# Sums of squares spread over dense tiles, and each head's output norm one step later, in a two-block transformer kernel on one core

## The chip, the cores and the metric

The kernel runs on one core of one Trainium2 chip. The metric is the device time of one execution in microseconds (us), the median over several executions; less is better. The core's engines are TensorE (PE in the profile; its weight loads are PEld), VectorE (DVE), ScalarE (ACT), GpSimd (POOL) and SyncE (SP, which issues most of the loads).

## The reference

512 tokens of width 1024 go through two transformer blocks. The change lies in the first, in its gated delta rule. Cut to what matters:

```python
qkv = silu(causal_dwconv(dn_qkv, dn_conv_w))           # dn_qkv: columns of h @ w_in + b_in
q, k, vv = split(qkv, [1024, 2048])                     # 8 heads of 128 each
q = q * rsqrt(sum(q * q, -1) + 1e-6)
k = k * rsqrt(sum(k * k, -1) + 1e-6)
beta, g = sigmoid(dn_b), -exp(dn_a_log) * softplus(dn_a + dn_dt_bias)
# chunks of 64 tokens: G = cumsum(g); a unit lower triangular system per chunk
lmat = where(strict, beta * (k k^T) * decay, 0)
sol  = triangular_solve(eye + lmat, [v * beta, k * beta * exp(G)])
o    = scan over the chunks (state, attention with decay)
o = o * rsqrt(mean(o * o, -1) + 1e-6) * dn_norm_w * silu(z)   # the head's output norm
```

The rest of the first block (spatial gating, merging, layer norms, a mixture of 32 experts) and the whole second block (attention, a recurrence, a feed-forward part) are not touched.

## The kernel before

Activations lie with the width on the 128 partitions and the 512 tokens along the row. The input projection is cut into 72 *dense tiles* `("d", n)` of 128 output columns by 512 tokens. A tile is 24 matmuls with 512 moving columns: for each k of 0 to 7 the three products of `exact` (high by low, high by high, low by high part of fp32 numbers). `p_dense` issues them; it is a generator that yields after k = 3, so that a tile can be taken in two halves. Tiles 0 to 23 are q, k and v of the heads: ACT copies a tile out of PSUM (`s_evac`), DVE does the convolution (`v_qkv`, three SCALAR_TENSOR_TENSOR on BG), ACT the SiLU and, for q and k, the square (`s_silu`; squares go to ST for the first eight, to M for the last eight, and `sq_done` counts them).

`p_sums(r, bank)` adds the squares up over the partitions: for four squares `m = 4r + y` and four groups of 128 tokens it takes the square as the stationary operand and one column of ones as the moving one. So 16 matmuls of one column, which the trace holds as 32 records (each fp32 matmul is two). ACT waits for the filled tile `("nc", r)` before it writes the next four squares.

Every engine's program is written out by hand, in order, with semaphore waits. `p_qk`, `s_qk`, `v_qk`, `g_qk` are the first stage (tiles 0 to 11). Then the eight heads run in pairs: `weave` takes one step of head h and of head h + 1 in turn, then one half dense tile (`p_dense1` and its partners), on each engine separately. `p_head`, `v_head`, `s_head`, `g_head` are the steps of one head; step 1 of `p_head` is `kb`, step 2 `kk` and `dt`, step 3 `at`, step 4 `eg`, then eight steps without work for the heads on PE. In these DVE does the 16-row triangular inverse by substitution, for both heads of a pair at once: `v_sub_turn` (one STREAM_TRANSPOSE of ST) opens it and `v_sub_rows` are 28 small operations that each wait for the one before. At its end `v_sub_spread` gives `xt0`, which PE waits for (`x0`, transposes L276 of cst,ST).

The norm of a head's output is its *tail*: `p_tail_sums` (4 one-column matmuls, 8 records, tile `on`), `v_tail_sums` (mean plus epsilon, sm<-ps,sm), `s_tail` (square root), `v_tail_spread` (reciprocal, then a 128x512 product ST<-cst,sm), `p_tail_scale` (tile `os`, ST,cst with 512 columns), `v_tail` (BG<-BG,pc,ps, 128x512). The tail of head h - 2 is done inside the first steps of head h; those of heads 6 and 7 in `p_merge`.

PSUM has eight banks; `B.tile(key, bank)` names a tile, and `room(t)` makes PE wait until the bank's last tile was drained. Dense tiles use banks 0 and 1 beside the heads, a pair's heads banks 2 to 4 and 5 to 7 (`b0 = 2 + 3 * (h % 2)`).

Of the kernel before, what the change touches and what calls it, by code (L numbers as in the profile page):

```python
# [17 lines left out]
P = 128  # L18
D = 1024
T = 512  # L20
NT = 4
# [148 lines left out]
def build(nc, a, cst_d, rope_d, out):  # L170
    ctx = ExitStack()
    with ctx:
# [57 lines left out]
        def four(x):  # L230
            return x.rearrange("p (c t) -> p c t", c=4)
# [23 lines left out]
        def tt(E, o, x, y, op):  # L255
            return E.e.tensor_tensor(o, x, y, op)  # L256
# [14 lines left out]
        def mm(o, l, r, start=True, stop=True):  # L271
            return p.e.matmul(o, lhsT=l, rhs=r, start=start, stop=stop, skip_group_check=True)  # L272
# [16 lines left out]
        hTp = (HTH, HTL)  # L289

        def exact(o, l, r, start, stop):
            mm(o, l[0], r[1], start=start, stop=False)
            mm(o, l[0], r[0], start=False, stop=False)
            return mm(o, l[1], r[0], start=False, stop=stop)

        def room(t):
            for x in t.room:
                p.wait_ge(*x)
# [347 lines left out]

        def p_dense(n, bank, rhs, kind):
            p.wait_ge(*split_done(("d", n)))  # L650
            t = B.tile(("d", n), bank, nr=2 if n < 24 else 1)
            room(t)
            x, hi, lo = parts(("d", n))
            for k in range(8):
                p.wait_ge(*split_done((kind, k)))
                z = exact(t.at, (hi[:, k, :], lo[:, k, :]), (rhs[0][:, k, :], rhs[1][:, k, :]), k == 0, k == 7)
                if k == 3:
                    yield
            z.then_inc(t.filled)
            w_used[n // 4] = [t.full()]  # L660
# [68 lines left out]
        def sq_at(m):  # L729
            return ST[:, m % 4, :] if m < 8 else M[:, m % 4, :]  # L730

        def p_sums(r, bank):
            t = B.tile(("nc", r), bank)
            room(t)
            for y in range(4):
                m = 4 * r + y
                p.wait_ge(sq_done, m + 1)
                for i in range(NT):  # L740
                    z = mm(t.at[:, 4 * i + y:4 * i + y + 1], sq_at(m)[:, i * P:(i + 1) * P], ones[:, 0:1])
            z.then_inc(t.filled)

        def heads4(x, r):
            return x[:, :, 4 * (r // 2):4 * (r // 2) + 4]
# [136 lines left out]
        def s_prep2():  # L882
# [4 lines left out]
            s.wait_ge(*t.full())  # L887
            act(eGr, t.at[0:32, 0:P], ACT.Exp).then_inc(t.drained)

        def p_qk():  # L890
            for n in range(12):
                for _ in p_dense(n, n % 4, hTp, "T"):
                    pass
                if n == 2:
                    p_ab()
                elif n == 5:
                    p_prep1()
                    p_sums(0, 6)
                elif n == 9:
                    p_prep2()  # L900
                    p_sums(1, 7)
            p_beta(1, 6)

        def s_qk():
# [140 lines left out]
        def p_head(h):  # L1045
            LT, C, X, XT, Y, AT = sets[h % 2]
            KG, KD, VB, VN = LT, C, X, Y
            q4, k4, v4 = four(Qr[:, h, :]), four(Kr[:, h, :]), four(Vr[:, h, :])
            b0 = 2 + 3 * (h % 2)
            p.wait_ge(*B["rb"].free())  # L1050
            p.wait_ge(*B["br", h // 4].free())
            p_spread(("kb", h), b0, h, btr[h // 4])
            if h > 1:
                p_tail_sums(h - 2)
            yield
            p.wait_ge(silu_done, qk_of(h))
            p.wait_ge(*B["kb", h].free())
            p_products(("kk", h), b0 + 1, lambda c: k4[:, c, :], lambda c: Y[:, c, :])
            p.wait_ge(gm_done, h + 1)
            p_products(("dt", h), b0 + 2, lambda c: X[:, c, :], lambda c: ule)  # L1060
            yield
            p_products(("at", h), b0, lambda c: k4[:, c, :], lambda c: q4[:, c, :])
            if h > 1:
                p_tail_scale(h - 2)
            yield
            p_spread(("eg", h), b0 + 2, h, eGr)
            yield
            for _ in range(8):
                yield
            p.wait_ge(xt0_done, h + 1)  # L1070
            p_turn4(("x0", h), b0 + 1, XT)
            yield
            p.wait_ge(*B["x0", h].free())
            for n in range(3):
                p.wait_ge(lc_done[h % 2], 3 * (h // 2) + n + 1)
                if n:
                    p.wait_ge(*B["xx", h, n - 1].free())
                p_half(("y", h, n), b0, C, firsts(X, n))
                yield
                p.wait_ge(*B["y", h, n].free())  # L1080
                p_half(("xt", h, n), b0 + 2, Y, seconds(XT, n))
                yield
                if n < 2:
                    p.wait_ge(*B["xt", h, n].free())
                    p_turn4(("xx", h, n), b0 + 1, XT)
                    yield
            p_turn4(("kt", h), b0, k4)
            p.wait_ge(silu_done, v_of(h))
            p_turn4(("vt", h), b0 + 1, v4)
            yield  # L1090
            p.wait_ge(*B["kt", h].free())
            p.wait_ge(*B["xt", h, 2].free())
            p_products(("w", h), b0 + 2, lambda c: KG[:, c, :], lambda c: XT[:, c, :])
            yield
            p.wait_ge(*B["vt", h].free())
            p.wait_ge(*B["w", h].free())
            S = Y[:, 3, :]
            ob = B.tile(("o", h), b0)
            room(ob)
            for c in range(4):  # L1100
                n2 = 2 if c < 3 else 1
                t = B.tile(("s", h, c), b0 + 1 + c % 2, nw=n2, nr=n2)
                room(t)
                cs = slice(c * P, (c + 1) * P)
                if c:
                    p.wait_ge(*B["s", h, c - 1].free())
                    mm(t.at[:, 0:P], XT[:, c, :], VB[:, c, :], stop=False)
                    mm(t.at[:, 0:P], KG[:, c, :], S, start=False).then_inc(t.filled)
                    mm(ob.at[:, cs], S, q4[:, c, :], stop=False)
                else:  # L1110
                    mm(t.at[:, 0:P], XT[:, c, :], VB[:, c, :]).then_inc(t.filled)
                yield
                vn = VN[:, c % 2, :]
                p.wait_ge(*t.free(1))
                z = mm(ob.at[:, cs], vn, AT[:, c, :], start=c == 0)
                if c == 3:
                    z.then_inc(ob.filled)
                else:
                    mm(t.at[:, P:2 * P], KD[:, c, :], vn).then_inc(t.filled)
                yield  # L1120
# [4 lines left out]
        fd_done, of_done = sem("o_scale_spread"), sem("o_scale")  # L1125

        def p_tail_sums(h):
            t, z = B.tile(("on", h), 4 + 3 * (h % 2)), sets[h % 2][3]
            room(t)
            p.wait_ge(hsq_done, h + 1)  # L1130
            for c in range(4):
                i = mm(t.at[:, c:c + 1], z[:, c, :], ones[:, 0:1])
            i.then_inc(t.filled)

        def p_tail_scale(h):
            t = B.tile(("os", h), 4 + 3 * (h % 2))
            room(t)
            p.wait_ge(fd_done, h + 1)
            mm(t.at, ones, sets[h % 2][3].rearrange("p c t -> p (c t)")).then_inc(t.filled)
# [23 lines left out]
        def v_head(h):  # L1163
# [4 lines left out]
            v.wait_ge(*t.full())  # L1168
            v.wait_ge(silu_done, qk_of(h))
            tt(v, Y, k4, four(t.at), MUL).then_inc(t.drained)  # L1170
            if h > 1:
                v_tail_sums(h - 2)
            yield
            if h > 1:
                v_tail_spread(h - 2)
            yield
            t = B["kk", h]
            v.wait_ge(*t.full())
# [4 lines left out]
            v.wait_ge(*t.full())  # L1183
            tt(v, AT, four(t.at), C, MUL).then_inc(t.drained)
            if h > 1:
                v_tail(h - 2)
            yield
            t = B["eg", h]
            v.wait_ge(*t.full())
# [1 line left out]
            tt(v, q4, q4, four(t.at), MUL).then_inc(t.drained)  # L1191
            v_sub_take(h)
            yield
            for i0, i1 in ((1, 5), (5, 8), (8, 10), (10, 12), (12, 14), (14, 15), (15, DB)):
                if h % 2:
                    if i0 == 1:
                        v_sub_turn(h)
                    v_sub_rows(h, i0, i1)
                    if i1 == DB:
                        v_sub_back()  # L1200
                yield
# [40 lines left out]

        def s_head(h):
            LT, C, X, XT, Y, AT = sets[h % 2]
            if h > 1:
                s_tail(h - 2)
            yield
            t = B["dt", h]
            s.wait_ge(*t.full())
            act(C, four(t.at), ACT.Exp).then_inc(t.drained)  # L1250
            for _ in range(11):
                yield
            t = B["x0", h]
            s.wait_ge(*t.full())
# [81 lines left out]

        def p_dense1():
            for n in range(12, 24):
                half = p_dense(n, n % 2, hTp, "T")
                next(half)  # L1340
                yield
                if n == 18 or n == 22:
                    p_sums(2 if n == 18 else 3, 1)
                yield from half
                yield
            for n in range(24, 32):
                half = p_dense_tok(n, n % 2)
# [2328 lines left out]
```

## Time and profile before

| | |
|---|---|
| runs of before | 2186.38, 2188.93, 2196.76 us; median 2188.93 |
| the profiled execution | 2186.67 us; span 2184.8 us, granted TensorE clock 0.945 |
| PE busy | 1991.2 us, 91% of the span |
| DVE busy | 951.7 us (44%) |
| ACT busy | 654.0 us (30%) |
| POOL busy | 434.0 us (20%) |
| first block up to the experts | about 0 to 750 us |
| experts | about 750 to 1270 us |

A profile is one execution. A row's times are us from the span's start. "Granted clock" is the share of full speed at which TensorE was allowed to run; 1.00 is 2.4 GHz and 0.50 is 1.2 GHz.

### The profile page before, as it was taken

Reading aid. Unit: us, or ns where it says so; the run is one execution under the profiler, and the core shown is the slowest. Engines: PE = TensorE matmul, PEld = TensorE weight load, DVE = VectorE, ACT = ScalarE, POOL = GpSimd, SP = SyncE. Lnnn points to the kernel's source line nnn. Section 1 sums busy time; section 2 is a strip of 40 time slices with the busy share of each in tenths; the row PEclk is TensorE's granted clock in tenths of the full one; section 3 lists DMA queues with packets and bytes.
Section 4 is the critical chain, followed back from the end, with each engine's and each line's share of the span. In section 5 each row is a group of like instructions: output and inputs, shape, how many; then the busy total and the mean of one; then the engine's idle time right before and its main releaser. Section 6 shows DMA issues by size and latency. Waiting matters only on the chain.

```text
span 2184.8 us, 22949 instructions
## 1 busy us (share of the span) xinstructions
PE 1991.2 (91%) x9520; PEld 1442.1 (66%) x9520; DVE 951.7 (44%) x1382; ACT 654.0 (30%) x981; POOL 434.0 (20%) x310
## 2 busy tenths in 40 slices
PE   7999989999999889787787889998879899999999
PEld 5887878888877733332333347676746687888787
DVE  7674475542535622110111155845635883222332
ACT  4554422424333101000000133352226753222221
POOL 5432131423326011111110022311003120000121
PEclk9898999999999889898998999999979899999999
DMA  4861423123244589999999953111201134232210
GB/s 164 258 158 49 97 58 78 39 77 57 60 149 182 201 326 405 403 406 407 407 409 411 417 202 116 39 49 49 68 29 39 39 126 154 95 98 98 96 58 39
DMA packets 97654, 361.02 MB, mean 165 GB/s; under 512 B 9850, under 2 KB 34588, under 8 KB 85256
## 3 DMA queue, kind: packets, MB, share of 16 engines
q1 hardware_dynamic: 86800, 335.14, 42.9%
q0 software_dynamic: 8240, 19.00, 2.5%
q10 hardware_dynamic: 2504, 5.35, 0.7%
q8 instruction: 78, 1.28, 0.2%
q14 instruction: 32, 0.26, 0.0%
HBM read 338.74 MB, written 29.10 MB: 168 GB/s over the span
## 4 chain that ended last, share of the span: by engine, by line
PE 78%; DVE 11%; ACT 5%; issue 4%; DMA 1%; POOL 0%; ACTq 0%; SPq 0%; DVEq 0%; POOLq 0%
PE ps L272 74%; PE ps L276 3%; DVE ST L256 2%; PE ps L2080 2%; DVE H L262 1%; ACT ST L268 1%; ACT L268 1%; DVE WL L256 1%; DVE BG L262 1%; DVE ST L994 1%; ACT M L268 1%; DVE sm L3017 0%; DVE BG L256 0%; DMA BG<-h1d,toki 0%; DVE ML L256 0%
## 5 line engine op out<-in xcount | busy, mean ns | idle before, releaser
L272 PE MATMUL ps<-XH,WS 128*128 128x512 f32 x704 | 218.7, 392 | 0.0
L272 PE MATMUL ps<-HTH,WL 128*128 128x512 f32 x448 | 180.0, 402 | 0.0
L272 PE MATMUL ps<-W,BG 128*64 128x512 f32 x496 | 160.2, 618 | 1.0 <-issue 1.0
L272 PEld LDWEIGHTS ps<-XH,WS 128*128 128x128 f32 x704 | 133.5, 190 | 28.1
L2187 DVE COPY BG<-ps 128x512 f32<-128x512 f32 x32 | 22.1, 692 | 288.7 <-PE ps L272 288.7
L266 ACT ACTIVATE BG<-ps 128x512 f32<-128x512 f32 x48 | 28.5, 595 | 373.5 <-PE ps L2080 339.9
L272 PE MATMUL ps<-XL,WS 128*128 128x512 f32 x352 | 138.3, 393 | 1.8 <-DVE XL L256 1.8
L272 PE MATMUL ps<-M,BG 128*64 128x512 f32 (+1 forms) x304 | 125.9, 559 | 7.3 <-ACT ST L266 7.3
L272 PE MATMUL ps<-X2H,GV 128*128 128x512 f32 (+1 forms) x512 | 129.6, 344 | 0.0
L272 PE MATMUL ps<-ST,BG 128*64 128x512 f32 (+2 forms) x416 | 102.5, 597 | 23.5 <-issue 22.7
L272 PE MATMUL ps<-WS,HH 128*128 128x512 f32 x352 | 109.5, 393 | 2.6 <-issue 2.6
L272 PE MATMUL ps<-BG 128*64 128x512 f32 (+2 forms) x256 | 93.4, 543 | 16.9 <-issue 16.9
L272 PE MATMUL ps<-U,BG 128*64 128x512 f32 x176 | 85.8, 644 | 22.4 <-issue 22.4
L272 PEld LDWEIGHTS ps<-HTH,WL 128*128 128x128 f32 x448 | 87.7, 196 | 19.7
L272 PE MATMUL ps<-X2L,GV 128*128 128x512 f32 (+1 forms) x256 | 95.8, 374 | 4.5 <-DVE H L262 4.1
L256 POOL TENSOR_TENSOR WS<-W,WS 128x1024 fp32r<-128x1024 f32 x11 | 26.3, 2393 | 366.9 <-ACT WS L266 366.9
L272 PEld LDWEIGHTS ps<-X2H,GV 128*128 128x128 f32 x512 | 89.6, 192 | 13.8 <-issue 2.7
L262 DVE SCALAR_TENSOR_TENSOR BG<-ST,pc,BG 128x512 f32<-128x512 f32 x72 | 75.7, 1052 | 51.3 <-ACT BG L266 49.4
L256 DVE TENSOR_TENSOR BG<-ps,ST 128x512 f32<-128x512 f32 x22 | 15.2, 692 | 180.9 <-PE ps L272 180.9
L268 ACT ACT_TABLE_LOAD x66 | 84.7, 1283 | 24.9 <-PE ps L272 19.4
L272 PEld LDWEIGHTS ps<-ST,BG 128*64 128x64 f32 (+1 forms) x416 | 40.9, 160 | 76.9 <-issue 75.7
L266 ACT ACTIVATE WS<-W 128x2048 fp32r<-128x2048 f32 (+1 forms) x44 | 65.3, 1484 | 80.9 <-PE ps L272 67.1
(394 smaller groups left out, 4443.3 us busy)
## 6 DMA issues: line engine op xcount, KB each, us to landing
W<-in_w SPq DMA_DIRECT2D x31, 2048.0 KB, 39.0
W<-in_w_in SPq DMA_DIRECT2D x27, 2048.0 KB, 9.9
ST<-in_w SPq DMA_DIRECT2D x21, 2048.0 KB
BG<-in_w SPq DMA_DIRECT2D x11, 2048.0 KB
U<-in_w SPq DMA_DIRECT2D x11, 2048.0 KB, 33.3
M<-in_w SPq DMA_DIRECT2D x11, 2048.0 KB, 37.8
HT<-in_w SPq DMA_DIRECT2D x11, 2048.0 KB
W<-in_w_ffn_in SPq DMA_DIRECT2D x22, 1024.0 KB, 7.7
```

The costliest lines, as they stand in the source:

```text
L256: return E.e.tensor_tensor(o, x, y, op)
L262: return v.e.scalar_tensor_tensor(out=o, in0=x, scalar=c, in1=y, op0=op0, op1=op1)
L266: return s.e.activation(o, x, f, scale=scale)
L268: return s.e.activation(o, x, f, bias=bias, scale=scale)
L272: return p.e.matmul(o, lhsT=l, rhs=r, start=start, stop=stop, skip_group_check=True)
L276: return p.e.transpose(o, x, ident[0:n, 0:n])
L994: v.e.tensor_reduce(o, z, AX.X, ADD, negate=True).then_inc(v.up())
L2080: z = p.e.transpose(t.at[:, k * BLK:(k + 1) * BLK], xg[j][:, k::8], ident[xg_at[j], xg_at[j]])
L2187: v.e.tensor_copy(hs[j], t.at).then_inc(t.drained)
```

## The change

Three things. The one-column sums of squares, 16 in one go, are cut into pieces of four (`p_sum(r, y, bank)`): in `p_qk` a table puts them behind tiles 3, 4, 5 and 7, 8, 9; in `p_dense1` they stand inside tiles 18 and 22, behind k = 1, 2, 3 and 4 of the eight. The tail's sums of head h - 2 move from behind `kb` to between `kk` and `dt`, and its later parts a step or two back on PE, DVE and ACT. The tiles `on` and `os` go to other banks (b0 and b0 + 1).

```diff
-        def p_dense(n, bank, rhs, kind):
+        def p_dense(n, bank, rhs, kind, between=()):
...
                 z = exact(t.at, (hi[:, k, :], lo[:, k, :]), (rhs[0][:, k, :], rhs[1][:, k, :]), k == 0, k == 7)
+                if k in between:
+                    p_sum(*between[k])
                 if k == 3:
                     yield
...
-        def p_sums(r, bank):
-            t = B.tile(("nc", r), bank)
-            room(t)
-            for y in range(4):
-                m = 4 * r + y
-                p.wait_ge(sq_done, m + 1)
-                for i in range(NT):
-                    z = mm(t.at[:, 4 * i + y:4 * i + y + 1], sq_at(m)[:, i * P:(i + 1) * P], ones[:, 0:1])
-            z.then_inc(t.filled)
+        def p_sum(r, y, bank):
+            if y == 0:
+                room(B.tile(("nc", r), bank))
+            t, m = B["nc", r], 4 * r + y
+            p.wait_ge(sq_done, m + 1)
+            for i in range(NT):
+                z = mm(t.at[:, 4 * i + y:4 * i + y + 1], sq_at(m)[:, i * P:(i + 1) * P], ones[:, 0:1])
+            if y == 3:
+                z.then_inc(t.filled)
...
+        SUMS_AFTER = {3: [(0, 0)], 4: [(0, 1)], 5: [(0, 2), (0, 3)], 7: [(1, 0)], 8: [(1, 1)], 9: [(1, 2), (1, 3)]}
...
                     p_prep1()
-                    p_sums(0, 6)
                 elif n == 9:
                     p_prep2()
-                    p_sums(1, 7)
+                for r, y in SUMS_AFTER.get(n, ()):
+                    p_sum(r, y, 6 + r)
...
             p_spread(("kb", h), b0, h, btr[h // 4])
-            if h > 1:
-                p_tail_sums(h - 2)
             yield
...
             p_products(("kk", h), b0 + 1, lambda c: k4[:, c, :], lambda c: Y[:, c, :])
+            if h > 1:
+                p_tail_sums(h - 2)
             p.wait_ge(gm_done, h + 1)
...
             p_products(("at", h), b0, lambda c: k4[:, c, :], lambda c: q4[:, c, :])
-            if h > 1:
-                p_tail_scale(h - 2)
             yield
             p_spread(("eg", h), b0 + 2, h, eGr)
             yield
+            if h > 1:
+                p_tail_scale(h - 2)
...
             tt(v, AT, four(t.at), C, MUL).then_inc(t.drained)
             if h > 1:
-                v_tail(h - 2)
+                v_tail_spread(h - 2)
             yield
...
             v_sub_take(h)
             yield
+            if h > 1:
+                v_tail(h - 2)
             for i0, i1 in ((1, 5), (5, 8), (8, 10), (10, 12), (12, 14), (14, 15), (15, DB)):
...
             act(C, four(t.at), ACT.Exp).then_inc(t.drained)
-            for _ in range(11):
+            yield
+            if h > 1:
+                s_tail(h - 2)
+            for _ in range(10):
                 yield
...
+                r = {18: 2, 22: 3}.get(n)
+                yield from p_dense(n, n % 2, hTp, "T", {k: (r, k - 1, 1) for k in range(1, 5)} if r else ())
```

What moves on the engines is seen in their orders. On PE at tile 22, the last twelve matmuls of a half, a step of two heads (128x64) and the sums (cst,M 128x1) stood so before:

```order
L272 MATMUL ps<-HTH,WL_52 128x512
L272 MATMUL ps<-ST 128x64 x8
L272 MATMUL ps<-cst,M 128x1 x16
L272 MATMUL ps<-HTL,WHM 128x512
L272 MATMUL ps<-HTH,WHM 128x512
L272 MATMUL ps<-HTH,WL_52 128x512
```

and after the change, from the second of the four pieces on:

```order
L272 MATMUL ps<-HTH_49,WL1_52 128x512
L272 MATMUL ps<-cst,M 128x1 x4
L272 MATMUL ps<-HTL_50,WHM_55 128x512
L272 MATMUL ps<-HTH_49,WHM_55 128x512
L272 MATMUL ps<-HTH_49,WL1_52 128x512
L272 MATMUL ps<-cst,M 128x1 x4
L272 MATMUL ps<-ST 128x64 x8
L272 MATMUL ps<-HTL_50,WHM_55 128x512
L272 MATMUL ps<-HTH_49,WHM_55 128x512
L272 MATMUL ps<-HTH_49,WL1_52 128x512
L272 MATMUL ps<-cst,M 128x1 x4
```

The block of 16 became pieces of four with three dense matmuls or the heads' step between them. On DVE, in the third to fifth step of heads 2 and 3 (COPY and BG<-BG,ps belong to `eg`, STREAM_TRANSPOSE opens the row substitution, BG<-BG,pc,ps is `v_tail`), before:

```order
L262 SCALAR_TENSOR_TENSOR BG<-BG,pc,ps 128x512
L387 BN_STATS sm<-H 128x6 x2
L389 BN_AGGR sm<-sm 128x2
L1190 COPY sm<-ps 128x4
L256 TENSOR_TENSOR BG<-BG,ps 128x512
L976 TENSOR_REDUCE ST<-ST 128x4x16
L1190 COPY sm<-ps 128x4
L256 TENSOR_TENSOR BG<-BG,ps 128x512
L976 TENSOR_REDUCE ST<-ST 128x4x16
L256 TENSOR_TENSOR H<-ps,ST 128x512
L980 STREAM_TRANSPOSE ST<-ST 128x512
```

and after, with the line numbers of the changed kernel:

```order
L1157 RECIPROCAL sm<-sm 128x4
L256 TENSOR_TENSOR ST<-cst,sm 128x512
L387 BN_STATS sm<-H 128x6 x2
L389 BN_AGGR sm<-sm 128x2
L1192 COPY sm<-ps 128x4
L256 TENSOR_TENSOR BG<-BG,ps 128x512
L980 TENSOR_REDUCE ST<-ST 128x4x16
L1192 COPY sm<-ps 128x4
L256 TENSOR_TENSOR BG<-BG,ps 128x512
L980 TENSOR_REDUCE ST<-ST 128x4x16
L256 TENSOR_TENSOR H<-ps,ST 128x512
L262 SCALAR_TENSOR_TENSOR BG<-BG,pc,ps 128x512 x2
```

The two `v_tail` now stand directly ahead of the STREAM_TRANSPOSE, and the two reciprocals with their 128x512 products where they were. On ACT in the same steps the square roots (sm<-sm 128x4) stood ahead of the exponentials (ST<-ps) and now stand behind them and behind a GELU (H<-H):

```order
L268 ACT_TABLE_LOAD
L268 ACTIVATE ST<-ps 128x512 x2
L268 ACT_TABLE_LOAD
L268 ACTIVATE H<-H 128x512
L268 ACT_TABLE_LOAD
L268 ACTIVATE sm<-sm 128x4 x2
L268 ACT_TABLE_LOAD
```

That is one more ACT_TABLE_LOAD for each of the three pairs that have a tail to do.

## Rows read from the trace of the kernel before

**Rows 1.** Stretches, TensorE alone: us, busy (instructions), granted clock, DMA share, GB/s

```profile
62.60:66.00 3.40, 3.40 (x29) 1.00 1.02 412
66.00:72.80 6.80, 6.80 (x24) 0.50 0.81 332
...
161.60:168.40 6.80, 6.80 (x23) 0.50 0.25 77
...
209.40:216.20 6.80, 6.80 (x22) 0.50 0.00 0
...
400.50:407.30 6.80, 6.80 (x24) 0.50 0.01 2
526.80:530.20 3.40, 3.40 (x23) 1.00 0.00 0
```

**Rows 2.** Two more stretches: the columns are those of all engines

```profile
96.70:103.50 6.80, 6.80 (x23) 5.83 (x23) 5.38 (x5) 4.35 (x7) 4.68 (x3) 0.50 1.03 417
...
784.00:1240.00 456.00, 394.72 (x1810) 157.29 (x1808) 59.22 (x121) 33.48 (x64) 54.80 (x56) 0.92 1.00 406
```

**Rows 3.** PE by time (start, us, line, what, count) at the first sums

```profile
63.15 0.39 PE L272 MATMUL ps<-HTH,WL 128*128 128x512 f32 x1
63.47 0.42 PE L276 MATMUL ps<-cst,ST 16*128 16x16 f32 x4
63.82 5.03 PE L272 MATMUL ps<-cst,ST 128*128 128x1 f32 x32
...
69.28 0.63 PE L272 MATMUL ps<-HTH,WHU 128*128 128x512 f32 x1
69.71 0.63 PE L272 MATMUL ps<-HTH,WL 128*128 128x512 f32 x1
```

**Rows 4.** PE by time at full clock: two dense products

```profile
202.63 0.40 PE L272 MATMUL ps<-HTH,WHM 128*128 128x512 f32 x1
202.86 0.39 PE L272 MATMUL ps<-HTH,WL 128*128 128x512 f32 x1
```

**Rows 5.** PE by time: eight one-column records at full clock, then `kb` spread

```profile
266.37 1.05 PE L272 MATMUL ps<-cst,ST 128*128 128x1 f32 x8
267.36 0.37 PE L272 MATMUL ps<-rb,cst 32*128 32x128 f32 x1
```

**Rows 6.** DVE by time: its wait for the tile behind the first sums

```profile
77.87 2.33 DVE L262 SCALAR_TENSOR_TENSOR BG<-ST,pc,BG 128x512 f32<-128x512 f32 x3 [8.09 <-ACT BG L266]
```

**Rows 7.** PE by time at the second sums, behind tile 9

```profile
93.64 0.41 PE L272 MATMUL ps<-sm,cst 128*128 128x32 f32 x2 [0.97 <-DVE sm L262]
...
94.32 4.97 PE L272 MATMUL ps<-cst,ST 128*128 128x1 f32 x32
99.14 0.77 PE L272 MATMUL ps<-HTL,WHU 128*128 128x512 f32 x1
```

**Rows 8.** ACT by time: the eighth square

```profile
96.74 0.63 ACT L268 ACTIVATE ST<-BG 128x512 f32<-128x512 f32 x1
```

**Rows 9.** PE by time: the wait behind the third sums

```profile
173.04 0.47 PE L276 MATMUL ps<-cst,ST 128*128 128x128 f32 x1 [4.00 <-DVE ST L256]
```

**Rows 10.** DVE by time, heads 2 and 3: the parts of the tails

```profile
271.81 0.17 DVE L1153 RECIPROCAL sm<-sm 128x4 f32<-128x4 f32 x1
272.01 0.69 DVE L256 TENSOR_TENSOR ST<-cst,sm 128x512 f32<-128x512 f32 x1
...
283.75 0.73 DVE L262 SCALAR_TENSOR_TENSOR BG<-BG,pc,ps 128x512 f32<-128x512 f32 x1
```

**Rows 11.** DVE by time: its wait for PE ahead of the substitution

```profile
289.89 0.69 DVE L256 TENSOR_TENSOR H<-ps,ST 128x512 f32<-128x512 f32 x1 [0.52 <-PE ps L272]
...
548.72 0.16 DVE L1190 COPY sm<-ps 128x4 f32<-128x4 f32 x1 [0.80 <-PE ps L272]
```

**Rows 12.** PE by time: `x0` of heads 2, 3, then of head 4

```profile
318.82 0.90 PE L276 MATMUL ps<-cst,ST 128*128 128x128 f32 x3 [4.64 <-DVE ST L256]
...
447.78 0.66 PE L276 MATMUL ps<-cst,ST 128*128 128x128 f32 x4 [0.20 <-DVE ST L256]
```

More of the change, by code:

```diff
@@ L1127, in p_tail_sums @@
         def p_tail_sums(h):
-            t, z = B.tile(("on", h), 4 + 3 * (h % 2)), sets[h % 2][3]
+            t, z = B.tile(("on", h), 2 + 3 * (h % 2)), sets[h % 2][3]
             room(t)
@@ L1135, in p_tail_scale @@
         def p_tail_scale(h):
-            t = B.tile(("os", h), 4 + 3 * (h % 2))
+            t = B.tile(("os", h), 3 + 3 * (h % 2))
             room(t)
@@ L1170, in v_head @@
             tt(v, Y, k4, four(t.at), MUL).then_inc(t.drained)
+            yield
             if h > 1:
                 v_tail_sums(h - 2)
-            yield
-            if h > 1:
-                v_tail_spread(h - 2)
             yield
@@ L1244, in s_head @@
             LT, C, X, XT, Y, AT = sets[h % 2]
-            if h > 1:
-                s_tail(h - 2)
             yield
@@ L1250, in s_head @@
             act(C, four(t.at), ACT.Exp).then_inc(t.drained)
-            for _ in range(11):
+            yield
+            if h > 1:
+                s_tail(h - 2)
+            for _ in range(10):
                 yield
@@ L1338, in p_dense1 @@
             for n in range(12, 24):
[L1339 to L1344, printed above, removed]
+                r = {18: 2, 22: 3}.get(n)
+                yield from p_dense(n, n % 2, hTp, "T", {k: (r, k - 1, 1) for k in range(1, 5)} if r else ())
                 yield
```

## The prediction

> **What bounds the kernel now.** I read four views. First the page: PE is busy 91% of the span, DVE 44%, so the time is PE's, plus what it waits, plus what its clock costs. Second the windows, which give the granted clock of a stretch. In the first block PE runs at 1.00, but falls to 0.50, that is from 2.4 to 1.2 GHz, for 6.8 us behind each of the four blocks of 16 one-column products [rows 1, 2], and once behind the tails of heads 2 and 3, at 400.5 [rows 1]. Drops that come with a wait of over 4 us, as at 173, are another matter. The reader is to see that ahead of 66.0 PE was busy in all of the 3.40 us [rows 1], so no idle time goes before that drop; what stands there is the last dense products and then the block that began at 63.82 [rows 3]. Third PE by time, for what a drop costs. Dense products of 512 columns start 0.43 us apart at half clock [rows 3] and 0.23 at full [rows 4]. So a stretch of 6.8 us at half does what 6.8 x 0.23 / 0.43 = 3.6 us would do, and 3.2 us are lost. Fourth the waits, which say where 3.2 us saved would be kept: PE waits for the end of DVE's substitution for 4.00 us at 173.04 [rows 9], 4.64 at 318.82 and 0.20 at 447.78 [rows 12]. Elsewhere in the first block PE does not wait for the heads by more than 1 us.
>
> **Sums 0, now behind tiles 3, 4 and 5.** Thin work beside dense costs a turn: the product behind the last dense one starts 0.32 us later instead of 0.23 [rows 3, 4], 0.09 each way, 0.18 per piece (that leaving thin work costs as much as entering it is an estimate). Three places instead of one: +0.36. If the clock now holds, -3.2, together -2.9. DVE waits here for PE's tiles by way of ACT, 8.09 us ahead of 77.87 [rows 6], so an earlier tile is used. Bounds: +0.4 (the drop only moves) and -2.9. I take -2.9, since pieces of eight records have the nearest like in [rows 5], eight records at full clock, and no drop followed there.
>
> **Sums 1, behind tiles 7, 8 and 9.** Before, PE waited 0.97 us at 93.64, issued the two pairs, then the block, and tile 10 began at 99.14 [rows 7], with 103.5 - 99.14 = 4.4 us of it at half clock [rows 2], 2.1 us lost. A piece of eight records takes about 0.9 us: 0.99 to the next product, turn included [rows 5]. After: all starts 2.9 earlier; the pieces behind tiles 7 and 8 add 2 x (0.9 + 0.18) = 2.1, so tile 9 ends at 92.6 - 2.9 + 2.1 = 91.8 (the end of tile 9 before is 93.64 - 0.97 = 92.67). DVE's result is there at 93.64 - 2.9 = 90.7, so the 0.97 is gone. The two pairs take 0.68 (94.32 - 93.64), to 92.5, the third piece to 93.4. The fourth needs the eighth square, which ends at 97.37 before [rows 8] and at 94.5 after: PE waits 1.1. Then 0.9, and tile 10 begins at 95.4: 3.7 earlier, 2.9 of them sums 0's. The rest, -0.8, and the clock: thin work and a wait stand from 91.8 to 95.4 almost without a dense product, so I expect the drop to stay, though half of its 3.2 us then lies on the wait and the thin work; some 1.6 are lost instead of 2.1. Together **-1.3**. Bounds: -2.9 if no drop, -0.3 if it costs 1 us more.
>
> **Sums 2, inside tile 18.** The drop at 161.6 [rows 1] is worth as much, less three extra pieces (0.5). But at 173.04 PE waits 4.00 us for DVE's chain [rows 9], which does not depend on tile 18. What is won makes the wait longer, to about 6.7. I take **0**. Without that cover it would be -2.7.
>
> **Sums 3, inside tile 22.** -3.2 for the clock [rows 1], and four pieces, each charged a turn, +0.7: **-2.5**. PE does not wait from there to 318.82, where the wait ends by DVE's chain, whose start hangs on PE's `kk` and `eg`. Bounds -2.7 and +0.7: two of the pieces stand beside the heads' 128x64 products, thin work too, so a drop may stay. I take the first, since three or twelve dense products stand between the pieces.
>
> **The tails' sums between `kk` and `dt`.** Before, the sums of two heads and two spreads lay together behind the last dense products, at 400.5 the clock fell [rows 1]; beside the sums at 266.37 [rows 5] and at 526.8 [rows 1] it didn't. In the new place products of 128 columns stand around them. I take the drop at 400.5 as gone, **-3.2**. Bounds: -3.2, and +6.4 if all three pairs get one.
>
> **The tails' later parts.** On DVE the two `v_tail`, 0.73 us each [rows 10], so 1.4, leave a place ahead of a wait for PE and go directly ahead of the STREAM_TRANSPOSE, with which the substitution opens. Queued behind it is all of `v_sub_rows`, and PE waits for its end. `v_tail_spread`, 0.17 + 0.69, takes the place of `v_tail`: 2 x (0.86 - 0.73) = 0.3. So 1.7 us go onto the chain. Against them, DVE waited there for PE: 0.52 us in heads 2 and 3, 0.80 in heads 6 and 7 [rows 11], and I take 0.80 for heads 4 and 5. PE reaches `eg` earlier, because the two 512-column products of `os` now stand behind it, so these waits go: 1.2 + 0.9 + 0.9 = **+3.0**. At heads 2 and 3 and at 4 and 5 PE waits for the chain's end already [rows 12], so it counts in full; at heads 6 and 7 there is no wait for `x0`, and 0.9 is an upper bound. All bounds: 0 (hidden) to 5.1 (no wait given back). One more ACT_TABLE_LOAD for each pair stands on ACT, which is busy 30%, and behind its exponentials: 0.
>
> **Sum.** -2.9 - 1.3 + 0 - 2.5 - 3.2 + 3.0 = -6.9, against the profiled execution's 2186.7: 2179.8. The median of the runs is 2.3 above it, so **2182.1**. Could the rest take it back? In 784 to 1240 the DMA share is 1.00 at 406 GB/s [rows 2]: loads bound that stage, not PE. But they start when PE frees their space, so the stage begins earlier by what the first block wins, and the gain is kept; I choose this, and no row shows it.
>
> The Trainium skill bears on the clock terms (TensorE: Matmul & The Clock Gate, Part 1): the clock is throttled unless activity releases it, and a monitor goes by how busy TensorE has been. By busy time in the records PE was never idle ahead of 66.0, which read narrowly would leave nothing for the spreading to repair; read as activity of the array, one-column products count for little, and the drops are theirs.
>
> **Rivals.** (1) All comes back: no drop at sums 1 (-1.6 more) and the tails' parts on DVE hidden (-3.0): 2182.1 - 4.6 = 2177.5. For it speaks that pieces as small as at 266.37 did not drop the clock; against it the measured waits for the chain. Chance 0.20. (2) Drops only move: two of those at sums 0, 3 and the tails recur, +6.4: 2188.5. The 128x64 step and the tails' new place speak for it. Chance 0.12. (3) The other side: the drops are not the sums' doing, but would come in these stretches anyway. Then the clock gives nothing back, and what stays is +0.4 at sums 0, -0.8 at sums 1, +0.7 at sums 3 and +3.0 on the chain: +3.3 instead of -6.9, 2192.3. It decides for slower if the clock gives back less than 3.3 us in all. Against it: five drops, each behind one-column work. The skill's rule read narrowly (same page and part) would point here. Chance 0.04. (4) PE comes late with `os`: on PE a half dense tile, 12 x 0.23 = 2.7 us, stands between steps, and DVE's `v_tail` waits for it with the substitution behind it. Three pairs: 3 x 2.7 = +8.1, 2190.2. Against it: the weave puts `os` one step behind `eg` on PE and `v_tail` one behind on DVE. Chance 0.05. The likeliest, with its own range 2178 to 2186: 0.59.
>
> **Range and chances.** 2175 leaves room for (1) with the sums' price at its low end; 2190 takes in (2) and nearly (4). Within 0.5% of 2188.9, about what a measurement of this kernel can tell from no change, lies 2178.0 to 2199.9. Faster by more: most of (1) and a little of the likeliest, 0.24. Slower by more needs (3) and (4) together and some: 0.03. Same: 0.73.
>
> **What the profile after should show.** Granted clock 1.00 in 66 to 73, 206 to 216 and 395 to 405, and a drop left near 93 to 100; if 0.50 stands there as long as before, the clock terms are wrong. Tile 10 begins near 95.4, behind a wait of 1 us for ACT. PE's wait at 173 grows to about 6.7. The wait for `x0` of heads 2 and 3 grows by about 1 us and more by what PE gains between; the STREAM_TRANSPOSE starts right behind two SCALAR_TENSOR_TENSOR BG<-BG,pc,ps that don't wait. If they wait for `os`, rival (4) holds. The prediction is wrong above all if drops come at the tails' new place, or if the experts' stage doesn't begin earlier.

## The result, and the profile after

The changed kernel took 2174.04 us in the median of 5 runs (2172.82 to 2179.03), the kernel before 2189.56 us (5 runs, 2186.38 to 2196.76). The ratio is 0.993, with a 95% interval of 0.9912 to 0.9949: 15.5 us less, where 6.8 were forecast, and 1 us under the stated range. Two later measurements gave 0.9952 (0.9937 to 0.9968; 2177.73 against 2188.05 us) and 0.9927 (0.9904 to 0.9949; 2175.63 against 2191.79 us). So the gain is 10 to 16 us. The ratios leave out three executions that were two to five times as slow (5429.81 us of the changed kernel, 8513.61 and 10939.63 us of the kernel before).

The profiled execution took 2172.82 us. The page of after has in its first lines:

```profile
span 2171.0 us, 22947 instructions
...
PEclk9999999999999899999899999999979999999999
```

The windows of after, PE alone (us, busy (instructions), granted clock, DMA share, GB/s), answer to [rows 1] and [rows 2]:

```profile
66.00:72.80 6.80, 6.80 (x38) 1.00 0.78 317
94.10:100.90 6.80, 6.68 (x20) 0.50 1.03 420
...
206.00:212.80 6.80, 6.80 (x48) 1.00 0.01 2
...
260.00:280.00 20.00, 20.00 (x134) 1.00 0.10 33
392.00:412.00 20.00, 20.00 (x135) 1.00 0.29 103
520.00:540.00 20.00, 20.00 (x134) 1.00 0.32 83
```

The reader sees that the clock stays at 2.4 GHz where sums 0 and 3 stand, and in and behind the tails' sums (here at 265 to 268.5, 398 to 401 and 525 to 528.5 us), and that the drop at sums 1 is left. PE by time there, in after, against [rows 7]:

```profile
91.22 0.30 PE L272 MATMUL ps<-sm,cst 128*128 128x32 f32 x2
...
91.79 1.05 PE L272 MATMUL ps<-cst,ST 128*128 128x1 f32 x8
94.22 1.87 PE L272 MATMUL ps<-cst,ST 128*128 128x1 f32 x8 [1.37 <-ACT ST L268]
95.94 0.77 PE L272 MATMUL ps<-HTL,WHU 128*128 128x512 f32 x1
```

The drop begins at 94.1, as PE's wait ends: the wait lies at full clock, and the fourth piece takes 1.87 us where the third took 1.05.

And PE's wait at the first substitution and the one of heads 2 and 3, against [rows 9] and [rows 12]:

```profile
170.08 0.90 PE L276 MATMUL ps<-cst,ST 128*128 128x128 f32 x3 [6.69 <-DVE ST L256]
...
312.98 2.22 PE L276 MATMUL ps<-cst,ST 128*128 128x128 f32 x8 [4.61 <-DVE ST L256]
```

To see where the time goes, the start of one and the same dense product in two traces is compared, again and again through the program. All numbers are us against the first profile of the kernel before (negative: earlier), at the time that the product has there. The row 50 lies ahead of all that the change touches, so what it shows is chance; at 75, sums 0 are done and sums 1 not begun. The product at 442 is the one at 441.75.

| product at | after | after_again | after_3 | after_4 | before_2 | before_3 | before_4 | before_5 | tails_only | sums_only |
|---|---|---|---|---|---|---|---|---|---|---|
| 50 | -0.1 | 0.5 | -1.4 | 0.1 | -0.2 | 0.8 | -0.7 | 0.0 | -0.5 | 1.5 |
| 75 | -3.2 | -2.6 | -4.5 | -1.4 | -0.2 | -0.8 | -2.3 | 0.0 | -0.5 | -1.6 |
| 111 | -2.9 | -3.9 | -4.5 | -4.3 | 0.1 | -0.8 | -2.2 | 0.3 | -0.3 | -2.8 |
| 202 | -2.8 | -5.0 | -4.4 | -7.6 | 0.4 | -0.8 | -2.2 | 0.5 | 0.0 | -2.6 |
| 230 | -5.9 | -8.1 | -7.5 | -6.7 | 0.3 | -0.8 | -2.2 | 0.5 | 0.0 | -5.7 |
| 389 | -5.9 | -7.5 | -6.0 | -6.1 | 3.8 | -0.8 | -2.1 | 3.9 | 0.1 | -5.7 |
| 442 | -9.4 | -10.9 | -9.5 | -9.6 | 3.8 | -0.8 | -2.2 | 3.9 | -3.4 | -5.7 |
| 619 | -8.6 | -10.2 | -8.7 | -8.8 | 6.9 | 2.3 | 1.0 | 7.0 | -2.6 | -2.5 |
| 740 | -8.0 | -10.6 | -8.2 | -8.3 | 7.5 | 2.1 | 0.8 | 6.6 | -2.9 | -2.8 |
| 2180 | -13.9 | -13.2 | -14.5 | -11.6 | 7.5 | -4.2 | -2.1 | 4.2 | -3.2 | -9.1 |

The column after is the first profile of the changed kernel. Of its 13.9 us, 8.0 come in the first block, and 5.9 behind 740 us, where the program is unchanged.

### The profile page after: what moved, and what is told of

Its sections match the earlier page's. It is cut to its first block, busy times and chain, and to the rows that moved or that the text cites. A ratio compares the mean times of both kernels' runs of the same rounds, so it can differ in the third digit from the quotient of the medians.

```text
span 2171.0 us, 22947 instructions
## 1 busy us (share of the span) xinstructions
PE 1974.8 (91%) x9520; PEld 1430.2 (66%) x9520; DVE 950.8 (44%) x1382; ACT 657.2 (30%) x984; POOL 433.5 (20%) x310
## 4 chain that ended last, share of the span: by engine, by line
PE 76%; DVE 13%; ACT 5%; issue 5%; DMA 1%; POOL 0%; ACTq 0%; SPq 0%; DVEq 0%; POOLq 0%
PE ps L272 71%; PE ps L276 3%; DVE ST L256 2%; PE ps L2081 2%; DVE H L262 1%; ACT ST L268 1%; ACT L268 1%; DVE BG L262 1%; DVE WL L256 1%; DVE ST L998 1%; ACT M L268 1%; DVE BG L256 1%; DVE sm L3018 0%; DVE ML L256 0%; ACT M L269 0%
## 5 line engine op out<-in xcount | busy, mean ns | idle before, releaser
L272 PEld LDWEIGHTS ps<-ST 128*128 128x128 f32 x672 | 84.5, 191 | 6.9 <-DVE ST L256 2.5
```

## Experiments

The theories were these. **1:** each stretch of the first block gives what its clock gives, and the difference behind 740 us is chance of one execution. **2:** the earlier start of the later stages brings gain there. **3:** the tails do it all. **4:** the later stages are faster for another reason, such as what the changed first block leaves behind. Of DVE's chain: **P**, the two products at its head delay `x0` by their length; **Q**, they cost nothing.

**One part of the change alone.** `sums_only` has the spread sums, and the tails as before; `tails_only` the reverse. The edit of `tails_only` against the changed kernel:

```diff
-        SUMS_AFTER = {3: [(0, 0)], 4: [(0, 1)], 5: [(0, 2), (0, 3)], 7: [(1, 0)], 8: [(1, 1)], 9: [(1, 2), (1, 3)]}
+        SUMS_AFTER = {5: [(0, 0), (0, 1), (0, 2), (0, 3)], 9: [(1, 0), (1, 1), (1, 2), (1, 3)]}
...
-                yield from p_dense(n, n % 2, hTp, "T", {k: (r, k - 1, 1) for k in range(1, 5)} if r else ())
+                half = p_dense(n, n % 2, hTp, "T")
+                next(half)
+                yield
+                if n == 18 or n == 22:
+                    for y in range(4):
+                        p_sum(2 if n == 18 else 3, y, 1)
+                yield from half
```

> The sums of squares spread as in the change, the tails as before. Theory 1 (gain is what each stretch shows, the later part's difference is chance of an execution): 2.3 + 0.7 + 0 + 3.1 = 6.1 us less before 400 us, then a clock drop near 395 again as before, so 6 us under the kernel before, and whatever the later stages add by chance. Theory 2 (a gain in the first block brings an equal one in the experts' stage and behind it): some 10 us less. Theory 3 (the tails do it): no gain.

> The tails as in the change, all four blocks of 16 one-column sums whole as before. Theory 1: the clock drops behind the four blocks are there, the one at 400.5 is gone, 3.5 less there and 1.1 lost again on the substitution chains: 2.4 us under the kernel before. Theory 2: some 4 us less. Theory 3: 10 us or more less.

Measured together, against 2188.05 us (30 runs) for the kernel before: sums_only 2180.83 us (ratio 0.9981, 0.9964 to 0.9998), tails_only 2180.4 us (0.9962, 0.9944 to 0.9979). Each part gives a gain of its own: 7.2 us for the sums, where theory 1 had 6, and 7.6 us for the tails, where theory 1 had 2.4. Most of the miss at the tails lies in the comparison: theory 1 counted against the first profile of the kernel before, and the runs of that kernel are slower than it where more drops come, as is shown below. Windows of tails_only, PE alone: the blocks are whole, and the drops behind sums 0, 1 and 3 are there; the three places of the tails (their sums stand here at 271 to 274.5, 404 to 407.5 and 531 to 534.5 us) are free of one.

```profile
66.30:73.10 6.80, 6.80 (x20) 0.50 0.68 276
97.00:103.80 6.80, 6.80 (x21) 0.50 1.02 415
209.70:216.40 6.70, 6.70 (x20) 0.50 0.00 0
...
266.00:286.00 20.00, 20.00 (x134) 1.00 0.10 34
398.00:418.00 20.00, 20.00 (x135) 1.00 0.29 101
526.00:546.00 20.00, 20.00 (x135) 1.00 0.32 86
```

Windows of sums_only:

```profile
66.00:72.80 6.80, 6.80 (x42) 1.00 0.98 399
...
206.00:212.80 6.80, 6.80 (x49) 1.00 0.01 2
394.90:401.70 6.80, 6.80 (x24) 0.50 0.01 2
524.60:531.40 6.80, 6.80 (x25) 0.50 0.00 0
```

The last line is the surprise: with the tails as before there is a drop at 524.6 that the first profile of the kernel before did not have at the same place [rows 1]. Theory 3 is out, since the sums alone give a gain too.

**The kernel before again.** Four more profiles of the unaltered kernel, to see how often such a cluster is followed by a drop.

> The kernel before, unaltered, for a second profile. Theory 1 (behind a block of 16 one-column sums the clock always falls, behind the tails' smaller cluster only in some executions): drops again near 66, 97, 161 and 209 us; among the three tail clusters near 266, 400 and 528 us, one or two drops, not the same as in the first profile. Theory 2 (the places are fixed by the program): drops at the same five places, none near 266 and 528.

> The kernel before once more. As for the second profile: theory 1 has drops behind all four blocks and a changing choice among the tail clusters; theory 2 exactly the first profile's five.

> The kernel before once more: drops behind all four blocks; at the three tail clusters (near 266, 400, 528 us) 1, 3 and 2 of three in the profiles so far, so here most likely two.

> The kernel before once more, the same: drops behind all four blocks, most likely two at the tail clusters. With none at all in this one and the one before, the tails' share of the gain would be as the prediction had it, one drop.

Their times were 2194.21, 2182.44, 2184.59 and 2190.84 us. In all four the clock fell at sums 0, 1, 2 and 3, in before_3 and before_4 at sums 0 for 3.4 us alone instead of 6.8. Behind the tail clusters it fell in three, two, two and three of three places. Windows of before_2:

```profile
268.10:274.90 6.80, 6.80 (x24) 0.50 0.04 16
404.70:411.40 6.70, 6.70 (x22) 0.50 0.01 2
534.40:541.10 6.70, 6.70 (x23) 0.50 0.00 0
```

With the first profile (one) and sums_only (two) that is 13 of 18. By place: heads 0 and 1 in 2 of 6, heads 2 and 3 in 6 of 6, heads 4 and 5 in 5 of 6. The first profile was the one with the fewest. At heads 2 and 3, where it had its drop, every profile had one; what it hid is the drop that heads 4 and 5 mostly have, and heads 0 and 1 sometimes.

**The changed kernel again**, three more profiles, two of them with timed runs.

> The changed kernel, unaltered, once more, for a second profile. Theory 1: the first block's landmarks come out as in the first profile within 0.5 us (7.9 us earlier at 740 us than in the kernel before), while the gain between 740 us and the end, 5.9 us in the first profile, moves by several us. Theory 2: both repeat.

> The changed kernel once more, for a third profile. No drop behind sums 0 and sums 3 and at the tails' new place (near 260, 394 and 521 us); at sums 1 a drop of one or two steps; landmark at 740 us between 7.5 and 10.6 us before that of the first profile of the kernel before. If the tails' new place drops too in one of the three, the tails' part of the gain is chance.

> The changed kernel beside the kernel before and the halves, timed. If the clusters of the tails in the kernel before drop two times in three: 10 to 12 us under it. If the first measurement (15.5 us) was right: 15 or more. In its profile no drop at the tails' new place, and at 740 us between 5 and 18 us ahead of any profile of the kernel before.

At the tails' new place none of the 4 x 3 clusters was followed by a drop, and none in the 7 other profiles of kernels with that part of the change: 0 of 33. Whether the place of the sums does it, or the later place of `os` and the other banks, no run tells apart. Behind 740 us the four profiles gained 5.9, 2.6, 6.3 and 3.3 us on the first profile of before; the kernel before itself, in its other four profiles, -0.1, 6.4, 2.9 and 2.5 us, and ran the same program there. The eight other profiles with some of the change, which run it too, lie between 2.4 us lost (chain_more) and 6.9 gained. The mean of all twelve is 3.3 us, that of the five of before 2.3, with the first profile's 0 counted. That is chance, as theory 1 has it, and a difference of 1 us isn't decided. The spread sums are not wholly safe. Windows of after_4:

```profile
68.10:71.50 3.40, 3.40 (x10) 0.51 0.93 382
93.00:99.80 6.80, 5.43 (x34) 1.00 1.00 399
201.20:211.40 10.20, 10.20 (x38) 0.50 0.00 0
156.80:167.00 10.20, 9.73 (x31) 0.50 0.16 51
```

Here the clock held at sums 1, and fell at the three others; the drop at sums 3 begins at 201.2, inside the pieces. That is rival 2 of the prediction in one execution, two of the drops back, and it took 2175.06 us. Over the nine profiles with sums 0 spread into pieces of four, a drop came there in one, against 6 of 6 with whole blocks; at sums 3 in 2 of 9, against 6 of 6; at sums 1 in 8 of 9, against 6 of 6.

**Cover for the shifted start.** `after_pad` puts 36 products ahead of dense tile 60:

```diff
+            if n == 60:
+                p.wait_ge(*split_done((kind, 0)))
+                for _ in range(12):
+                    exact(t.at, (hi[:, 0, :], lo[:, 0, :]), (rhs[0][:, 0, :], rhs[1][:, 0, :]), True, True)
```

> The changed kernel with 36 products of 512 columns added ahead of dense tile 60 (their sums are overwritten), 36 x 0.227 = 8.2 us of TensorE near 560 us, so that all behind it stands where it stood in the kernel before. Theory 1 (gain is the first block's alone): back at the kernel before, within 1 or 2 us. Theory 2 (the later gain follows from the earlier start of the later stages): back at the kernel before too, and the later stages take as long as in it. Theory 4 (the later stages are faster for another reason, such as what the changed first block leaves behind): still 6 us under the kernel before.

2182.98 us, ratio 0.9974 (0.9959 to 0.9988). At 740 us its profile stands 0.4 us behind the first one of before, so the 8.2 us are all paid, and at 2180 us it is 6.5 ahead. It was 6.9 us faster in the later stages with no earlier start, where the unaltered kernel was 6.4 faster in before_3, so nothing speaks for theory 2. In the medians it is 5.1 us under the kernel before: not theory 1's "within 1 or 2 us", and near theory 4's 6. But theory 1's number came from the 7.9 us of the first profile. At 740 us the mean of the five profiles of before stands 3.4 us behind the first, so after_pad starts the later stages 3.0 us ahead of the typical execution; the 2.1 us that are left are less than the later stages differ by chance. Theory 4 isn't needed, and isn't ruled out to the last microsecond.

**DVE's chain.** `no_vtail` shortens the two products at its head to 4 of 512 columns, so most of the heads' output is not normed; `chain_more` opens the substitution three times:

```diff
-            stt(o, o, pcol(NWC), t.at, MUL, MUL).then_inc(t.drained)
+            stt(o[:, 0:4], o[:, 0:4], pcol(NWC), t.at[:, 0:4], MUL, MUL).then_inc(t.drained)
```

```diff
+            for _ in range(2):
+                v.e.transpose(ROWS_L, LANES).then_inc(v.up())
+                v.wait_ge(*v.now)
             v.e.transpose(ROWS_L, LANES).then_inc(v.up())
```

> The changed kernel, the norm's last product (BG<-BG,pc,ps) done on 4 of 512 columns only, so that most of the heads' output is left unscaled. Theory P (the prediction's step: the two products at the head of the substitution chain delay x0 by their length): x0 of the pairs comes some 1.1 us earlier against the products before it, in the pairs 2,3 and 4,5. Theory Q (they cost nothing, since DVE had waited elsewhere): x0 not earlier by over 0.3 us.

> The changed kernel with the STREAM_TRANSPOSE that opens the substitution done three times (same output each time): 1.3 to 1.6 us more on DVE at the head of the chain, in all four pairs. Theory P: PE's wait for x0 grows by as much in the pairs 0,1, 2,3 and 4,5 (in 6,7 by nearly as much), 5 to 6 us in all at 656 us. Theory Q: no growth.

Each theory is right in one run and wrong in the other. Read from the product at 241 us to that at 619 us: no_vtail goes from 6.17 to 10.22 us ahead of before, after from 5.90 to 8.60, so 1.35 us are gained. For heads 2 and 3, `x0` comes 1.1 us earlier than in after by this measure, as P says, of which a longer drop of the clock behind it takes 0.4 back; the rest comes at heads 4 and 5. chain_more adds 1.5 us to each of the three chains between these products, and goes from 8.84 to 10.66, where after_again goes from 8.09 to 10.16: 0.25 us lost of 4.5, as Q says. Only in the pair 0,1, ahead of 241 us, does `x0` come 1.1 us later. What takes it up stands in the timeline, in no wait. DVE in after, where the chain of heads 2 and 3 opens (the second row is the two `v_tail`):

```profile
282.95 0.68 DVE L256 TENSOR_TENSOR H<-ps,ST 128x512 f32<-128x512 f32 x1
283.55 1.39 DVE L262 SCALAR_TENSOR_TENSOR BG<-BG,pc,ps 128x512 f32<-128x512 f32 x2
284.86 0.70 DVE L984 STREAM_TRANSPOSE ST<-ST 128x512 f32<-128x512 f32 x1
285.67 2.08 DVE L259 TENSOR_SCALAR ST<-ST 128x2 f32<-128x2 f32 x1
287.78 0.17 DVE L256 TENSOR_TENSOR ST<-ST 128x8 f32<-128x8 f32 x1
```

and POOL at the same time:

```profile
285.32 2.39 POOL L256 TENSOR_TENSOR WL<-W,WHU 128x1024 fp32r<-128x1024 f32 x1 [1.03 <-ACT WHU L266]
```

A TENSOR_SCALAR of two columns took 2.08 us, and ended at 287.75, when POOL's split of a weight tile ended (285.32 + 2.39 = 287.71). In the kernel before the same split held another step of the chain:

```profile
292.12 0.17 DVE L994 TENSOR_REDUCE ST<-ST 128x6 f32<-128x18 f32 x1
292.32 2.40 DVE L256 TENSOR_TENSOR ST<-ST 128x32 f32<-128x32 f32 x1
...
292.27 2.40 POOL L256 TENSOR_TENSOR WL<-W,WHU 128x1024 fp32r<-128x1024 f32 x1 [1.65 <-ACT WHU L266]
```

and in chain_more, with the transpose three times, the hold shrinks instead of the chain growing:

```profile
281.92 1.46 DVE L985 STREAM_TRANSPOSE ST<-ST 128x512 f32<-128x512 f32 x2
283.42 0.71 DVE L987 STREAM_TRANSPOSE ST<-ST 128x512 f32<-128x512 f32 x1
284.24 0.58 DVE L259 TENSOR_SCALAR ST<-ST 128x2 f32<-128x2 f32 x1
...
282.39 2.39 POOL L256 TENSOR_TENSOR WL<-W,WHU 128x1024 fp32r<-128x1024 f32 x1 [1.03 <-ACT WHU L266]
```

The Trainium skill has a rule for it (SBUF — State Buffer, Terms): VectorE and GpSimd share one pair of ports, which one holds for a full instruction while the other is blocked. The trace agrees: all three held operations end within 0.1 us of POOL's. No run takes the split away, so that it holds DVE is read from these ends. So what stands at the head of the chain is free up to the end of POOL's split, and what would have been done before the split is done behind it. In the pair 2,3 the split itself also came 1.0 us earlier than the rest of PE's work did (285.32 against 292.27 is 6.95, PE 5.9), since the product H<-ps,ST ahead of it no longer waits 0.52 us for PE, nor stands behind the `v_tail`: ACT takes its result, then copies WHU, and POOL's split waits for that copy. The two cancel: PE's wait is 4.61 us, before 4.64.

The same is seen at heads 6 and 7, where the split (POOL, 544.63, 2.40 us) holds a TENSOR_SCALAR of two columns for 1.60 us at 545.46. At heads 4 and 5 it isn't `x0` that PE pays for most, but a weight tile, whose low part DVE splits in the same queue:

```profile
433.13 0.50 PE L272 MATMUL ps<-UL,WHS 128*128 128x512 f32 x1 [0.41 <-DVE WL L256]
```

Of the 0.8 us that after loses between 442 and 619, 0.7 are lost at this wait and just behind it. Before had none there, and no_vtail has none.

**Other sizes.** `sums1_later` puts sums 0 behind tiles 3 to 6 and sums 1 behind 8, 9 and 10; `halves` and `halves_timed`, the same kernel twice, have pieces of eight products instead of four.

```diff
-        SUMS_AFTER = {3: [(0, 0)], 4: [(0, 1)], 5: [(0, 2), (0, 3)], 7: [(1, 0)], 8: [(1, 1)], 9: [(1, 2), (1, 3)]}
+        SUMS_AFTER = {3: [(0, 0)], 4: [(0, 1)], 5: [(0, 2)], 6: [(0, 3)], 8: [(1, 0)], 9: [(1, 1)], 10: [(1, 2), (1, 3)]}
```

```diff
+        SUMS_AFTER = {4: [(0, 0), (0, 1)], 5: [(0, 2), (0, 3)], 8: [(1, 0), (1, 1)], 9: [(1, 2), (1, 3)]}
...
+                yield from p_dense(n, n % 2, hTp, "T", {1: [(r, 0, 1), (r, 1, 1)], 5: [(r, 2, 1), (r, 3, 1)]} if r else ())
```

> The changed kernel with sums 0 behind tiles 3, 4, 5 and 6 one piece each, and sums 1 one tile later (8, 9 and twice behind 10). If the fourth piece's wait for the eighth square (1.4 us) and the thin work beside it cause the drop that is left near 94 us: no wait, clock 1.00 throughout 60 to 125, tile 11 begins 1.4 + 1.6 = 3 us earlier than in the changed kernel, and the whole is 2 to 3 us faster. If the drop there comes from the sums of the prepared gates (the two pairs behind tile 9) or the gain is taken back by the wait at 170 us: no difference at 176 us.

> The changed kernel with each block of 16 in two halves of eight (16 records, 1.8 us) instead of pieces of four. If the clock falls by the share of thin work in a stretch: no drops at 66 and 209 either, and the kernel like the changed one, with 0.2 to 0.7 us fewer turns. If only pieces of four are small enough: drops come back behind some of the halves, 3.2 us each.

> The kernel with halves of eight, timed. If its one look (2166.8 us) was no chance: 3 to 7 us under the changed kernel in the same call, since no drop comes near 94 us and the fourth piece waits less. If it was chance: within 2 us of the changed kernel. Its profile tells how often a half brings a drop: in the first there was one step at 66.6 and one at 155.3.

sums1_later took 2173.8 us, ratio 0.9939 (0.9917 to 0.9961), not told apart from the changed kernel. Its PE by time behind tile 9:

```profile
91.25 0.41 PE L272 MATMUL ps<-sm,cst 128*128 128x32 f32 x2 [1.48 <-DVE sm L262]
```

The wait for the square is gone, and PE waits for DVE's result instead, 1.48 us, as it did before the change; 3.4 us of half clock are left at 93.3. At 176 us it is 5.6 us ahead of before, against 3.0 to 6.5 in the four profiles of the changed kernel, so the hoped-for 3 us are not shown. The halves took 2166.84 us in a single run; in six runs they take 2175.13 us beside 2175.63 us for the changed kernel, measured together, so the first was chance, and four or eight make no difference that was measured. Drops with halves: 3.4 us each at 66.6 (sums 0) and 155.3 (sums 2) in the first profile, 6.8 us at 93.3 in the second, none at sums 3. Nor do turns show, of which pieces of four have twice as many: from 202 to 230 us, across sums 3 without a drop, halves gain 3.1 us on before, and after gains 3.1 too.

## Why the prediction was wrong

By its own steps: against the first profile of after (differences of the table), and then the mean of the four profiles of after against the mean of the five of before:

| step | predicted | first profile | means | how read |
|---|---|---|---|---|
| chance ahead of the change | | -0.1 | -0.2 | at 50 us |
| sums 0 | -2.9 | -3.1 | -2.0 | 50 to 75 us |
| sums 1 | -1.3 | +0.3 | -1.1 | 75 to 111 us |
| sums 2 | 0 | +0.2 | -1.1 | 111 to 202 us |
| sums 3 | -2.5 | -3.1 | -2.1 | 202 to 230 us |
| tails, both terms | -0.2 | -2.7 | -5.9 | 230 to 619 us |
| behind the change | | +0.6 | +0.4 | 619 to 740 us |
| sum | -6.9 | -8.0 | -12.2 | at 740 us |

**What failed first: the sentence "I take the drop at 400.5 as gone, -3.2".** The mechanism was right, but the term was sized by one profile in which one of three clusters had dropped. [rows 1] shows only that profile, and 526.8 free of a drop in it was read as a property of the place. It was a draw: 13 of 18 clusters drop. Over the five profiles of the kernel before it is 11 of 15, 2.2 in each, so the term is 2.2 x 3.2 = 7.0 us, 3.8 more than forecast. The same error sat in "the median of the runs is 2.3 above it": most of that difference is the chance of the drops, and it was carried over to the changed kernel, which no longer has those at the tails.

**Second: the +3.0 for the tails' later parts**, of which 0.8 was measured in the first profile. It was worked out from waits and lengths of instructions; the hold by POOL stands in the busy time of one small instruction and so in no wait. For heads 2 and 3 `x0` comes at most 0.1 us later against the product at 241 in the four profiles of after, so nothing of the 1.2 came by the chain. But in the three later ones 0.5 to 1.5 us are lost behind it (the table from 230 to 389), 0.7 in the mean of the four: there the drop of the clock that comes with this wait is longer (6.8 us instead of 3.4), or begins 1.6 us behind the wait's end instead of just ahead of it. The 0.8 came at heads 4 and 5 (0.9 predicted) in all four, but most of it by a wait for a weight tile and not for `x0`, so its size agrees by luck. At heads 6 and 7 nothing of the 0.9 stays.

**Third, in the first profile: sums 1**, +0.3 instead of -1.3. The step that failed is "half of its 3.2 us then lies on the wait and the thin work; some 1.6 are lost". The drop began only as the wait ended, and lay on work alone: 0.8 us lost on the fourth piece (1.87 instead of 1.05) and 2.3 on tile 10 (95.94 to 100.9), which began 3.2 us earlier than before and not 3.7. That the mean, -1.1, is near the forecast is luck: the drop lasted 6.8, 3.4, 6.8 and 0 us in the four profiles.

With the first two put right the tails come to -0.2 - 3.8 - 1.5 = -5.5, where -5.9 was measured. The four sums together, with what was chance ahead of them, give -6.6 at 230 us, where -6.7 was forecast; but that agreement is the sum of terms that miss by up to 1.1 each. At sums 0, two profiles of before had a drop half as long, and one of after had one. The turns that were charged with 0.18 us for each piece (0.36 at sums 0, 0.7 at sums 3; the -2.9 should read -2.8) cost 0.1 us or less in each block: behind a piece the next product starts 0.32 us later instead of 0.23, but at its start the second record follows the first after 0.03 us instead of 0.11. The timed gains of 15.5, 10.3 and 16.2 us lie around the 12.2.

Sums 2 is hidden behind PE's wait in the first profile, as forecast (6.69 us, 6.7 predicted). It isn't always: after_4 gains 3.3 us between 111 and 202. PE ran at half clock from 156.8 to 167.0 there, its wait shrank to 0.98 us, and `x0` itself came 1.3 us earlier against the product at 111. DVE's convolution in after, and in after_4:

```profile
162.29 4.29 DVE L262 SCALAR_TENSOR_TENSOR BG<-ST,pc,BG 128x512 f32<-128x512 f32 x3
...
160.94 2.32 DVE L262 SCALAR_TENSOR_TENSOR BG<-ST,pc,BG 128x512 f32<-128x512 f32 x3
```

In after, as in before (4.35 us at 165.19), a split of POOL (162.90 to 165.24) overlaps this group, which takes 2.0 us more than in after_4, where the split came at 164.17, behind it. The late split overlaps a later operation of DVE instead, which takes 0.7 us more. By this reading, up to 2 us of what the prediction took as the length of this chain are of the same kind as the hold at heads 2 and 3.

The rest held. At sums 1 the drop was left, behind a wait of 1.37 us for ACT (1.1 predicted). Rival 1, all drops gone and the chain hidden, was nearest, though the drop at sums 1 is not gone in three profiles of four and the chain hidden but for 0.8 us. Rival 2 is real as a rate, 1 of 9 and 2 of 9, not as a rule. Rival 3 is out: with whole blocks the clock fell in 18 of 18 cases at sums 0, 1 and 3, and in the program with spread sums in 11 of 27, 8 of them at sums 1. Rival 4 is out: the two `v_tail` don't wait for `os`. The later stages kept the gain, as the prediction chose: none of the four profiles of after gave any of it back behind 740 us.

## What to carry to other kernels

A clock drop in one profile is a sample. Before a term is sized by one, take several profiles of the same kernel, count how often each place drops, and price the place by its rate; the difference of one profile from the median is part of the same draw. Thin work (here products of one column) mostly keeps the clock when it is cut and set between dense products: 3 drops in 18 cases at sums 0 and 3, but 8 in 9 at sums 1, where a wait of PE and other small products stand beside the pieces. The cut itself cost 0.1 us or less a block. It pays where PE is the bound; behind a wait of PE (here 4.0 us) little or nothing comes of it. And look for held instructions: one whose duration is ten times its neighbours' is a wait that the list of waits doesn't show.

## What the hardware showed unexpectedly

The clock fell with TensorE busy in every microsecond of the records: in or right behind 32 one-column records (5 us, the last part at the lower clock) in 24 of 24 blocks at sums 0 to 3 in six profiles, and in or behind clusters of 16 of them between 16 spreads in 13 of 18. Cut into pieces of 8 records with dense products between them, the same work dropped it in 1 of 9 profiles at sums 0 and 2 of 9 at sums 3. Execution times of one unaltered kernel lay between 2179.03 and 2194.76 us in one measurement (30 runs), and profiles of it differed by up to 7.5 us at 740 us, most of which are these drops. VectorE operations of 2 to 50 columns took up to 2.4 us beside a split of GpSimd, and ended when it ended.
